# A decoder-layer kernel: other orders of the start-up work on ScalarE, VectorE and TensorE

## The chip, the core and the metric

The kernel runs on one core of a Trainium2 chip. The metric is the device time of one execution in microseconds; the median of 3 runs of the kernel before is 1664.91 us (1664.87 to 1665.24). All data are float32 but for a few masks.

## What is computed

One layer of a decoder on 1024 tokens of width 1024. First an RMSNorm, then projections, two attention mixers, a residual, a second RMSNorm, a mixture of 32 experts, a residual and a last RMSNorm. What the change touches is the first norm and the first use of its result:

```python
def rmsnorm(x, g):
    xf = x.astype(jnp.float32)
    y = xf * lax.rsqrt(jnp.mean(xf * xf, axis=-1, keepdims=True) + RMS_EPS)
    return y.astype(x.dtype) * g

hn = rmsnorm(h, norm_mix[l])
proj = xn @ w_in          # xn is hn; w_in is cut into blocks of 128 columns
```

## The kernel before

Each engine has its own instruction stream, written out by hand; semaphores order them. TT = 8 token tiles of P = 128 tokens are worked on one after the other in the head, and KT = 8 is the width in steps of 128.

The head, until the first projection, goes as follows. SyncE (SP) issues the loads in one queue: x tiles 0 to 3, the two halves of weight block 0, x tiles 4 and 5, weight block 1, x tiles 6 and 7, then further weights. GpSimd (POOL) makes constants (the identity `ident`, the column `eps_t` of epsilons, masks), and raises `const_ready` when the identity is done. ScalarE (ACT) waits for `const_ready`, then for each x tile takes the sum of squares (L885, with the read of the accumulator) and the root of the mean plus epsilon (L887, `std_done`). VectorE (DVE) takes the reciprocal (L1057), scales the tile into one of two buffers `xs` (L1060, `xs_ready`), and, when TensorE has turned the tile, takes it out of PSUM with the norm's gain into `hnT` (L1066, `hnT_done`). TensorE (PE) turns a scaled tile by 8 transposes of 128x128 (L555, `xT_ps`), in the function `turn_tokens`.

The order of VectorE's loop: for i = 0 to 8, scale tile i (if i < 8), then take tile i-1 (if i >= 1). Scaling tile i waits for `std_done` of tile i, and from i = 2 on for the transposes of tile i-2, since there are two `xs` buffers.

The order on TensorE: turn tiles 0 to 3; projection job 0 (L586; weight block 0 by tokens 0 to 511; 8 matmuls, each two instructions in the records, so 16), which waits for `hnT_done` of 4 tiles and for weight block 0; turn tiles 4 and 5; job 1 (weight block 1 by the same tokens, 16 instructions); turn tiles 6 and 7; job 2, which waits for all 8 tiles of `hnT`. From there on the projections follow one another (L586, L581), then attention, the output projection and the experts, whose matmuls (L834) have 64 stationary columns, two of them side by side at output partitions 0 and 64.

SyncE also waits for `xs_ready` of all 8 tiles before it issues the load of `w1c` (L420), which is first used some 100 us into the kernel.

Of the kernel before, what the change touches and what calls it, by code (L numbers as in the profile page):

```python
# [28 lines left out]
ALU = mybir.AluOpType  # L29
ACT = mybir.ActivationFunctionType  # L30
X = mybir.AxisListType.X

P = 128
# [10 lines left out]
TT = SEQ // P  # L44
KT = D // P
# [3 lines left out]
EPS = 1e-5  # L49
# [40 lines left out]
def build(nc, t, out):  # L90
    ctx = ExitStack()

    def sb(name, shape, dt=F32):
        return ctx.enter_context(nc.sbuf_tensor(name, shape, dt))

    def sem(name):
        return ctx.enter_context(nc.semaphore(name))
# [17 lines left out]
    def wa(a, b, pat=None, /, **kw):  # L115
        v = WA[:, a:b]
        return v.rearrange(pat, **kw) if pat else v

    def ba(a, b, pat=None, /, **kw):
        v = BA[:, a:b]  # L120
        return v.rearrange(pat, **kw) if pat else v

    hnT = wa(0, 8192, "p (k t) -> p k t", k=KT)
# [9 lines left out]
    xt = [wa(10496 + 1024 * i, 11520 + 1024 * i) for i in range(5)] + [wa(22528, 23552), wa(23552, 24576), ba(13312, 14336)]  # L133
# [8 lines left out]
    xs = ba(17408, 19456, "p (b n) -> p b n", b=2)  # L142
# [13 lines left out]
    ident = sb("ident", [P, P])  # L156
# [4 lines left out]
    gT = sb("gT", [P, KT])  # L161
# [10 lines left out]
    eps_t = sb("eps_t", [P, 1])  # L172
    stat = sb("stat", [P, 3, TT])
# [4 lines left out]
    esk = sb("esk", [P, 4, 2])  # L178
# [5 lines left out]
    PS = ctx.enter_context(nc.psum_tensor("PS", [P, 8, 512], F32))  # L184
# [6 lines left out]
        m_in0 m_in1 merge_ps gate_act merge_dve wout_in gff_in xr_in0 xr_in1 out_ps h2_done h2_std  # L191
        hn2_done h2T_ps h2T_done log_ps log_done zero_done routed scattered hn_st ids_in rows_due row_col row_ps row_tab ids_held slotx_done slots_done wr_in
        we0 we1 we2 we3 we4 we5 we6 we7 we8 x_blk x_tr xT_evac mm1 mm3 tanh_done hid_done hT_ps hT_done y_ps y_evac y_st
        g_in0 g_in1 fin_in0 fin_in1 fin_in2 fin_in3 fin_in4 fin_in5 fin_in6 fin_in7 g_in2 g_in3 g_in4 g_in5 g_in6 g_in7 comb_std comb_done out_st0 out_st1 act_step h2_st0 h2_st1 gate_in gw_in0 gw_in1 gst0 gst1 hu_done loop_left gelu_arg tanh_gates nsink_done comb_sum gfin_in assigned wdiag_done fin_ps wr_ready sel_done first_ps first_ids route_arg route_exp route_ps masks_ready tables y_free""".split()
    S = {n: sem(n) for n in names}
    block = ctx.enter_context(nc.Block())

# [8 lines left out]
    NBLK = len(blocks)  # L206

    jobs = [(name, c, hf) for c, (name, _, _) in enumerate(blocks) for hf in range(2)]
    jobs = [jobs[0], jobs[2], jobs[1], jobs[3]] + [("vg", 0, i) for i in range(TT)] + jobs[4:]
    job_of = {c: j for j, (name, c, h) in enumerate(jobs) if name != "vg" and h == 1}  # L210
# [60 lines left out]
    xT_ps = PS[:, 7, :].rearrange("p (c h n) -> p c h n", c=4, h=2)  # L271
# [268 lines left out]
    def _(pe):  # L540
# [8 lines left out]
        def turn_tokens(i):  # L549

            pe.wait_ge(S["xs_ready"], i + 1)
            if i >= 2:
                pe.wait_ge(S["hnT_done"], i - 1)
            for k in range(KT):
                mm = pe.transpose(PS[:, 4 + 2 * (i % 2) + k // 4, P * (k % 4):P * (k % 4) + P],  # L555
                                  xs[:, i % 2, P * k:P * k + P], ident[:, :])
            mm.then_inc(S["xT_ps"], 1)

        for i in range(4):
            turn_tokens(i)  # L560

# [11 lines left out]
        for j, (name, c, h) in enumerate(jobs):  # L573
# [3 lines left out]
            if name == "vg":  # L577
                if h == 0:
                    pe.wait_ge(S["vg_in"], 64)
                for k in range(KT):  # L580
                    mm = pe.matmul(PS[:, j % 4, 0:VG_W], hnT[:, k, P * h:P * h + P], vgw[:, k, :],  # L581
                                   start=(k == 0), stop=(k == KT - 1))
            else:
                pe.wait_ge(S[f"w_in{c % 6}"], 32 * (c // 6 + 1))
                for k in range(KT):
                    mm = pe.matmul(PS[:, j % 4, :], ws[:, c % 6, k, :], hnT[:, k, 512 * h:512 * h + 512],  # L586
                                   start=(k == 0), stop=(k == KT - 1))
# [11 lines left out]
            if j == 19:  # L599
                pe.wait_ge(S["gelu_dve"], 1)  # L600
                for ht in range(2):
                    mm = pe.matmul(PS[0:DH, 4, 0:126], w2c[:, 0, ht, :], gel[:, 2, 126 * ht:126 * ht + 126],
                                   start=(ht == 0), stop=(ht == 1))
# [122 lines left out]
        for dt in range(KT):  # L726
            for hf in range(2):
# [10 lines left out]
                for j, o in enumerate((qa, qb)):  # L738
                    for r in range(REP):
                        mm = pe.matmul(PS[:, b0 + j, :], wbr[:, dt % 2, 4 * j + r, :], o[:, r, sl],  # L740
                                       start=(r == 0), stop=(r == REP - 1))
# [120 lines left out]
        for j in range(TT // 2):  # L862
            i = 2 * j
# [5 lines left out]
            for c in range(2):  # L869
                for n in range(2):  # L870
                    mm = pe.matmul(PS[:, 2 * j + n, :], wdiag[:, j, c, :], fin_y[:, i, c, 512 * n:512 * n + 512],
                                   start=False, stop=(c == 1))
# [4 lines left out]
    def _(act):  # L877

        act.dma_start(gT[:, :], t["norm_mix"].rearrange("(k p) -> p k", p=P), allow_slow_non_contiguous=True) \
            .then_inc(S["gT_in"], 16)  # L880
        act.wait_ge(S["const_ready"], 1)

        for i in range(TT):
            act.wait_ge(S[f"x_in{i}"], 16)
# [91 lines left out]
        for i in range(TT + 1):  # L976
            if i >= 1:
                m = i - 1
# [64 lines left out]
    def _(dve):  # L1043
        steps = [0]

        def step(ins):

            steps[0] += 1
            ins.then_inc(S["dve_step"], 1)
            dve.wait_ge(S["dve_step"], steps[0])  # L1050


        dve.wait_ge(S["gT_in"], 16)
        for i in range(TT + 1):
            if i < TT:
                dve.wait_ge(S["std_done"], i + 1)
                step(dve.reciprocal(stat[:, 2, i:i + 1], stat[:, 1, i:i + 1]))  # L1057
                if i >= 2:
                    dve.wait_ge(S["xT_ps"], i - 1)
                dve.tensor_scalar(xs[:, i % 2, :], xt[i], stat[:, 2, i:i + 1], None, ALU.mult) \  # L1060
                    .then_inc(S["xs_ready"], 1)
            if i >= 1:
                m = i - 1
                dve.wait_ge(S["xT_ps"], m + 1)
                src = PS[:, 4 + 2 * (m % 2):6 + 2 * (m % 2), :].rearrange("p a (k n) -> p (a k) n", n=P)
                dve.tensor_tensor(hnT[:, :, P * m:P * m + P], src, gT[:, :].unsqueeze(2).to_broadcast([P, KT, P]),  # L1066
                                  ALU.mult).then_inc(S["hnT_done"], 1)

        def blocks_plus_pos(w):

# [129 lines left out]
        for pi in range(2 * KT):  # L1200
            b0, m, b, sl = 2 * (pi % 4), pi % 2, pi // 2 % 2, slice(512 * (pi % 2), 512 * (pi % 2) + 512)
# [56 lines left out]
        for i in range(TT + 1):  # L1258
# [5 lines left out]
            if i < TT:  # L1264
# [6 lines left out]
                src = PS[:, 2 * (i % 2):2 * (i % 2) + 2, :].rearrange("p a n -> p (a n)")  # L1271
# [15 lines left out]
        for k in range(5):  # L1287
            src, far_by = sums[k % 2], 2 ** k
# [60 lines left out]
        for n in range(TT + 1):  # L1349
# [4 lines left out]
            i = n - 1  # L1354
# [7 lines left out]
    def _(pool):  # L1362
        steps = [0]

        def step(ins):
            steps[0] += 1
            ins.then_inc(S["pool_step"], 1)
            pool.wait_ge(S["pool_step"], steps[0])

        g = nc.gpsimd  # L1370
        step(g.memset(ident[:, :], 0.0))
        step(g.memset(eps_t[:, :], EPS))
        step(g.memset(ones[:, :], 1.0))
        step(g.memset(tri[:, :], 1.0))
        step(g.memset(winmask[:, :], 0.0))
# [138 lines left out]
```

## Time and profile before

| | |
|---|---|
| median of 3 runs | 1664.91 us |
| the profiled execution | 1666.44 us |
| its span, first to last instruction | 1664.6 us |
| TensorE busy | 1561.5 us (94%) |
| VectorE, ScalarE, GpSimd busy | 559.3, 347.9, 295.4 us |
| mean granted clock of TensorE | 0.981 |
| start of job 0, job 2 in the span | 21.22, 42.42 us |

Times in the profile are microseconds from the start of the span. "Busy" on TensorE counts an instruction until its modelled end, so consecutive ones overlap; the distance from start to start tells the rate. The granted clock is 1.00 at 2.4 GHz and 0.50 at 1.2 GHz. The chain of waits follows what released each step, back from the end of the stretch.

### The profile page before, as it was taken

The page shows a single profiled execution, that of the slowest core. Times are in us where ns is not written, and L with a number is a line of the kernel's source. Part 1 is how long each engine was busy: PE and PEld are TensorE (multiplying, and loading weights), DVE is VectorE, ACT ScalarE, POOL GpSimd, SP SyncE. Part 2 cuts the span into 40 slices and gives each one's busy share as a digit, 9 for nine tenths or more (in the row PEclk, how much of TensorE's full clock was granted, in tenths as well). Part 3 has the DMA queues.
Part 4 walks back from the last instruction along what each step waited for, and adds up shares of the span by engine and source line. Part 5 has one row for each costly group of instructions (what it writes and reads, how often), then busy time and mean ns, then how long its engine had stood idle before and what let it go on. Part 6 is the DMA issues. An engine that isn't in the chain of part 4 may idle for free.

```text
span 1664.6 us, 21601 instructions
## 1 busy us (share of the span) xinstructions
PE 1561.5 (94%) x7605; PEld 841.6 (51%) x7606; DVE 559.3 (34%) x1538; ACT 347.9 (21%) x859; POOL 295.4 (18%) x434
## 2 busy tenths in 40 slices
PE   6999998999999999998999999699799999999995
PEld 3454544444444454444444555466366666666652
DVE  3201003766666656654222345411011111111115
ACT  3000002444343443433000111111111111111113
POOL 2000001322222222222001011221112121212113
PEclk9999999999999999998999999699999999999998
DMA  9205540453111111102443831599999999999938
GB/s 233 66 5 104 73 136 28 163 188 133 45 28 30 45 33 26 45 13 89 164 140 108 338 115 69 206 411 415 424 415 422 393 363 406 419 419 418 418 127 309
DMA packets 135977, 332.11 MB, mean 200 GB/s; under 512 B 39224, under 2 KB 79576, under 8 KB 126704
## 3 DMA queue, kind: packets, MB, share of 16 engines
q1 hardware_dynamic: 117472, 297.98, 49.1%
q0 software_dynamic: 10048, 21.32, 3.7%
q10 hardware_dynamic: 8400, 12.07, 2.1%
q8 instruction: 33, 0.54, 0.1%
q14 instruction: 24, 0.20, 0.0%
HBM read 276.09 MB, written 55.25 MB: 199 GB/s over the span
## 4 chain that ended last, share of the span: by engine, by line
PE 79%; DMA 8%; DVE 6%; issue 2%; ACT 1%; POOL 1%; SPq 1%; POOLq 0%; ACTq 0%; DVEq 0%
PE PS L834 15%; PE PS L702 12%; PE PS L586 11%; PE PS L848 8%; PE PS L740 7%; PE PS L775 6%; PE PS L688 4%; PE PS L649 4%; DMA WA<-w 4%; PE PS L668 4%; PE PS L581 3%; DMA BA<-hn_d,ids 1%; DMA ids<-ids_d 1%; PE PS L811 1%; PE PS L760 1%
## 5 line engine op out<-in xcount | busy, mean ns | idle before, releaser
L702 PE MATMUL PS<-WA 128*128 128x512 f32 x512 | 254.9, 611 | 2.2 <-ACT WA L944 1.6
L834 PE MATMUL PS<-WA,BA 128*64 128x256 f32 x2048 | 232.2, 384 | 4.7 <-DMA WA<-w 3.7
L834 PEld LDWEIGHTS PS<-WA,BA 128*64 128x64 f32 x2048 | 174.9, 139 | 69.3 <-issue 20.6
L586 PE MATMUL PS<-WA,BA 128*128 128x512 f32 x416 | 182.2, 599 | 5.4 <-DVE WA L1066 5.4
L1408 POOL TENSOR_SCALAR BA<-BA,rin,gates 128x640 f32<-128x640 f32 (+7 forms) x128 | 99.6, 781 | 270.7 <-DVE rin L1174 270.7
L1322 DVE SCALAR_TENSOR_TENSOR BA<-BA,PS 128x256 f32<-128x256 f32 x46 | 19.4, 421 | 347.1 <-ACT BA L1006 347.1
L586 PEld LDWEIGHTS PS<-WA,BA 128*128 128x128 f32 x416 | 79.3, 192 | 103.6 <-issue 97.7
L848 PE MATMUL PS<-WA,BA 128*64 128x512 f32 x512 | 117.8, 600 | 10.3 <-DVE BA L1332 8.4
L668 PEld LDWEIGHTS PS<-ident,BA 128*128 128x128 f32 x648 | 79.3, 144 | 94.1 <-issue 86.5
L702 PEld LDWEIGHTS PS<-WA 128*128 128x128 f32 x512 | 84.6, 190 | 78.5 <-issue 67.6
L934 ACT ACTIVATE BA<-PS,ngm 128x640 f32<-128x640 f32 (+7 forms) x128 | 89.9, 702 | 130.4 <-DVE ngm L1152 126.1
L775 PE MATMUL PS<-BA 128*128 128x512 f32 x256 | 113.1, 595 | 2.3 <-DVE BA L1210 2.3
L668 PE MATMUL PS<-ident,BA 128*128 128x128 f32 x648 | 101.2, 281 | 10.8 <-ACT BA L912 5.5
L740 PE MATMUL PS<-WA 128*128 128x512 f32 x256 | 110.1, 592 | 0.7 <-ACT WA L957 0.7
L834 PE MATMUL PS<-BA 128*64 128x256 f32 x896 | 99.7, 379 | 3.6 <-DMA BA<-w 3.6
L1184 DVE COPY BA<-PS 128x512 f32<-128x512 f32 (+3 forms) x126 | 62.7, 507 | 104.8 <-PE PS L668 104.7
L1151 DVE TENSOR_REDUCE mx<-PS 128x1 f32<-128x640 f32 (+7 forms) x128 | 90.6, 708 | 4.4
L834 PEld LDWEIGHTS PS<-BA 128*64 128x64 f32 x896 | 76.3, 137 | 30.4 <-issue 6.7
L1402 POOL TENSOR_TENSOR BA<-BA,rin 128x512 f32<-128x512 f32 (+1 forms) x32 | 31.5, 986 | 336.4 <-DVE rin L1161 336.4
L649 PE MATMUL PS<-WA 64*128 64x512 f32 (+3 forms) x384 | 75.8, 499 | 7.7 <-DVE pc L1142 4.0
L740 PEld LDWEIGHTS PS<-WA 128*128 128x128 f32 x256 | 48.6, 190 | 62.3 <-issue 60.7
L1474 POOL COPY ids<-ids 128x1 int32<-128x1 int32 x46 | 8.4, 183 | 399.6 <-PE PS L811 278.9
(238 smaller groups left out, 1524.9 us busy)
## 6 DMA issues: line engine op xcount, KB each, us to landing
WA<-w SPq DMA_DIRECT2D x66, 2048.0 KB, 24.9
BA<-w SPq DMA_DIRECT2D x30, 2048.0 KB, 27.9
rows_d<-WA SPq DMA_DIRECT2D x8, 2048.0 KB, 8.7
rows_d<-BA ACTq DMA_DIRECT2D x92, 128.0 KB
WA<-w_in SPq DMA_DIRECT2D x16, 512.0 KB, 5.4
gates_d<-WA SPq DMA_DIRECT2D x32, 256.0 KB, 2.4
WA<-gates_d SPq DMA_DIRECT2D x8, 1024.0 KB, 6.3
BA<-w_in SPq DMA_DIRECT2D x26, 256.0 KB, 5.6
```

The source lines that it names most:

```text
L586: mm = pe.matmul(PS[:, j % 4, :], ws[:, c % 6, k, :], hnT[:, k, 512 * h:512 * h + 512], start=(k == 0), stop=(k == KT - 1))
L649: mm = pe.matmul(PS[:, bank, 0:e - a], qb[rows, h, q], kz[rows, w, k0 + a:k0 + e], start=True, stop=True)
L668: mm = pe.transpose(PS[:, 4 + n % 2, P * m:P * m + P], src, ident[:, :])
L688: mm = pe.matmul(PS[DH * g:DH * g + DH, bank, :], v_sb[:, w, kb, DH * g:DH * g + DH], pT[:, SLOT0[br] + n, g, :, :], start=(br == "A" and ...
L702: mm = pe.matmul(PS[:, 6, :], gw[:, j, k, :], hnT[:, k, 512 * hf:512 * hf + 512], start=(k == 0), stop=(k == KT - 1))
L740: mm = pe.matmul(PS[:, b0 + j, :], wbr[:, dt % 2, 4 * j + r, :], o[:, r, sl], start=(r == 0), stop=(r == REP - 1))
L775: mm = pe.matmul(PS[:, 2 * (i % 2) + n, :], mT[:, i, k, :], wout[:, k, 512 * n:512 * n + 512], start=(k == 0), stop=(k == KT - 1))
L834: mm = pe.matmul(PS[DH * h:DH * h + DH, bank, 0:256], xT[:, k, :], w[par][:, k, 256 * h:256 * h + 256], start=(k == 0), stop=(k == KT - 1))
L848: mm = pe.matmul(PS[DH * n:DH * n + DH, 3, :], hT[:, j, SLOTS * h:SLOTS * h + SLOTS], W2[par][:, 2 * h + j, 512 * n:512 * n + 512], start= ...
L934: last = nc.scalar.activation(PB[:, n % 3, 0:nk], src, ACT.Exp, bias=ngm[:, v, 0:1], scale=SC, accum_out=den[:, v, 0:1])
L1151: step(dve.tensor_reduce(mx[:, v, 0:1], s[:, 0:nk], X, ALU.max))
L1408: last = g.tensor_scalar(pr, pr, rin[:, v, 0:1], gates[:, i, col:col + 1], ALU.mult, ALU.mult)
```

## The change

- GpSimd writes `eps_t` first, with a semaphore `eps_ready` of its own, ahead of the identity. ScalarE waits for this and no longer for `const_ready`, and takes one root of the epsilon column into a scratch element of `esk`, before it waits for the first x tile.
- TensorE, between `const_ready` and the first tile's transposes, multiplies the identity by itself: 6 rounds of 2 matmuls with 64 stationary columns, and 6 rounds of 4 with 32, each with 256 moving columns (the identity read twice), into a bank of PSUM that nothing else uses at that time. That is 36 matmuls.
- VectorE's loop is split. Tiles 0 to 3 are as before. From i = 4 on it takes tile i-1 first, and then scales tile i. The orders on the other engines stay.

```diff
+        wide = ident[:, :].unsqueeze(1).to_broadcast([P, 2, P])
+        for width in (64, 32):
+            for _ in range(6):
+                for c in range(0, P, width):
+                    pe.matmul(PS[c:c + width, 0, 0:2 * P], ident[:, 0:width], wide, start=True, stop=True)
         for i in range(4):
             turn_tokens(i)
...
-        act.wait_ge(S["const_ready"], 1)
+        act.wait_ge(S["eps_ready"], 1)
+        nc.scalar.activation(esk[:, 0, 0:1], eps_t[:, :], ACT.Sqrt)
...
-        for i in range(TT + 1):
-            if i < TT:
-                dve.wait_ge(S["std_done"], i + 1)
-                step(dve.reciprocal(stat[:, 2, i:i + 1], stat[:, 1, i:i + 1]))
-                if i >= 2:
-                    dve.wait_ge(S["xT_ps"], i - 1)
-                dve.tensor_scalar(xs[:, i % 2, :], xt[i], stat[:, 2, i:i + 1], None, ALU.mult) \
-                    .then_inc(S["xs_ready"], 1)
+
+        def scale_tokens(i):
+
+            dve.wait_ge(S["std_done"], i + 1)
+            step(dve.reciprocal(stat[:, 2, i:i + 1], stat[:, 1, i:i + 1]))
+            if i >= 2:
+                dve.wait_ge(S["xT_ps"], i - 1)
+            dve.tensor_scalar(xs[:, i % 2, :], xt[i], stat[:, 2, i:i + 1], None, ALU.mult).then_inc(S["xs_ready"], 1)
+
+        def take_tokens(m):
+
+            dve.wait_ge(S["xT_ps"], m + 1)
+            src = PS[:, 4 + 2 * (m % 2):6 + 2 * (m % 2), :].rearrange("p a (k n) -> p (a k) n", n=P)
+            dve.tensor_tensor(hnT[:, :, P * m:P * m + P], src, gT[:, :].unsqueeze(2).to_broadcast([P, KT, P]),
+                              ALU.mult).then_inc(S["hnT_done"], 1)
+
+        for i in range(4):
+            scale_tokens(i)
             if i >= 1:
-                m = i - 1
-                dve.wait_ge(S["xT_ps"], m + 1)
-                src = PS[:, 4 + 2 * (m % 2):6 + 2 * (m % 2), :].rearrange("p a (k n) -> p (a k) n", n=P)
-                dve.tensor_tensor(hnT[:, :, P * m:P * m + P], src, gT[:, :].unsqueeze(2).to_broadcast([P, KT, P]),
-                                  ALU.mult).then_inc(S["hnT_done"], 1)
+                take_tokens(i - 1)
+        for i in range(4, TT):
+            take_tokens(i - 1)
+            scale_tokens(i)
+        take_tokens(TT - 1)
...
         g = nc.gpsimd
+        g.memset(eps_t[:, :], EPS).then_inc(S["eps_ready"], 1)
         step(g.memset(ident[:, :], 0.0))
-        step(g.memset(eps_t[:, :], EPS))
```

## Rows read from the trace of the kernel before

**Rows 1.** The page: the chain of work that ended last, by engine.
```profile
PE 79%; DMA 8%; DVE 6%; issue 2%; ACT 1%; POOL 1%; SPq 1%; POOLq 0%; ACTq 0%; DVEq 0%
```

**Rows 2.** Chain of waits, 12 to 24 us; columns: start, us, what.
```profile
6.24 11.31 DMA WA<-x
...
19.28 0.75 DVE BA L1060
20.03 1.14 DVE WA L1066
...
21.22 2.93 PE PS L586 x3
```

**Rows 3.** Chain of waits, 24 to 60 us.
```profile
30.48 1.75 PE PS L555 x16
...
39.10 0.89 PE PS L555 x8
...
40.01 2.37 DVE WA L1066 x2
...
42.42 14.00 PE PS L586 x32
```

**Rows 4.** Timeline of ACT; columns: start, us, instruction, [idle before, releaser].
```profile
4.70 1.28 ACT L885 ACT_TABLE_LOAD   x1 [4.70 <-DMA WA<-x]
...
7.16 1.28 ACT L887 ACT_TABLE_LOAD   x1
...
8.66 1.04 ACT L885 ACTIVATE BA<-WA 128x1024 f32<-128x1024 f32 x1
```

**Rows 5.** Timeline of DVE.
```profile
10.15 0.17 DVE L1057 RECIPROCAL stat<-stat 128x1 f32<-128x1 f32 x1 [0.15 <-ACT stat L887]
...
12.12 1.22 DVE L1066 TENSOR_TENSOR WA<-PS,gT 128x1024 f32<-128x1024 f32 x1 [0.92 <-PE PS L555]
...
13.45 0.75 DVE L1060 TENSOR_SCALAR BA<-WA,stat 128x1024 f32<-128x1024 f32 x1
14.12 1.22 DVE L1066 TENSOR_TENSOR WA<-PS,gT 128x1024 f32<-128x1024 f32 x1
...
16.11 1.22 DVE L1066 TENSOR_TENSOR WA<-PS,gT 128x1024 f32<-128x1024 f32 x1
```

**Rows 6.** Timeline of PE: the head, and two short stretches at 11.3 and 16.6 us.
```profile
10.15 3.65 PE L555 MATMUL PS<-ident,BA 128*128 128x128 f32 x16 [10.15 <-DVE BA L1060]
14.27 1.57 PE L555 MATMUL PS<-ident,BA 128*128 128x128 f32 x8 [0.47 <-DVE BA L1060]
16.26 1.09 PE L555 MATMUL PS<-ident,BA 128*128 128x128 f32 x8 [0.42 <-DVE BA L1060]
...
11.24 1.06 PE L555 MATMUL PS<-ident,BA 128*128 128x128 f32 x4
...
16.42 0.82 PE L555 MATMUL PS<-ident,BA 128*128 128x128 f32 x6
```

**Rows 7.** PE busy and granted clock by stretch; the clock stands after the count.
```profile
18.00:18.50 0.50, 0.00 (x0) 1.00 1.27 282
18.50:19.00 0.50, 0.00 (x0) 0.71 1.34 231
...
25.50:26.00 0.50, 0.50 (x2) 0.96 1.18 325
...
41.00:42.40 1.40, 0.00 (x0) 1.00 1.00 327
42.40:44.00 1.60, 1.58 (x4) 1.00 1.06 336
```

**Rows 8.** Timeline of POOL: the last step of the identity.
```profile
3.07 0.29 POOL L1378 TENSOR_SCALAR_AFFINE_SELECT ident<-ident 128x128 f32<-128x128 f32 x1 [0.24 <-POOL cmpmask L1377]
```

**Rows 9.** Chain of waits, 1100 to 1120 us: a run of 64-column matmuls.
```profile
1111.72 6.91 PE PS L834 x64
```

**Rows 10.** DMA, issues at 2.32, 3.38, 11.56 and 24.01 us: KB, us to landing.
```profile
WA<-x SPq DMA_DIRECT2D x1, 512.0 KB, 8.7
...
BA<-w_in SPq DMA_DIRECT2D x1, 256.0 KB, 12.9
...
BA<-w_in SPq DMA_DIRECT2D x1, 256.0 KB, 9.7
...
BA<-w_in SPq DMA_DIRECT2D x1, 96.0 KB, 6.5
```

More of the change, by code:

```diff
@@ L193, in build @@
         we0 we1 we2 we3 we4 we5 we6 we7 we8 x_blk x_tr xT_evac mm1 mm3 tanh_done hid_done hT_ps hT_done y_ps y_evac y_st
-        g_in0 g_in1 fin_in0 fin_in1 fin_in2 fin_in3 fin_in4 fin_in5 fin_in6 fin_in7 g_in2 g_in3 g_in4 g_in5 g_in6 g_in7 comb_std comb_done out_st0 out_st1 act_step h2_st0 h2_st1 gate_in gw_in0 gw_in1 gst0 gst1 hu_done loop_left gelu_arg tanh_gates nsink_done comb_sum gfin_in assigned wdiag_done fin_ps wr_ready sel_done first_ps first_ids route_arg route_exp route_ps masks_ready tables y_free""".split()
+        g_in0 g_in1 fin_in0 fin_in1 fin_in2 fin_in3 fin_in4 fin_in5 fin_in6 fin_in7 g_in2 g_in3 g_in4 g_in5 g_in6 g_in7 comb_std comb_done out_st0 out_st1 act_step h2_st0 h2_st1 gate_in gw_in0 gw_in1 gst0 gst1 hu_done loop_left gelu_arg tanh_gates nsink_done comb_sum gfin_in assigned wdiag_done fin_ps eps_ready wr_ready sel_done first_ps first_ids route_arg route_exp route_ps masks_ready tables y_free""".split()
     S = {n: sem(n) for n in names}
```

## The prediction

> **What bounds the kernel now.** First the page's chain: TensorE carries 79% of it, so a microsecond that TensorE loses or gains in the head reaches the end, unless something later waits for a clock time of its own [rows 1]. Then the chain of waits of the head, to see who lets job 0 start. Before 17.55 it is the load of x tile 4 (issued 6.24, landing 11.31 later), and behind it VectorE: it scales tile 4 (19.28), and only then takes tile 3 (20.03); job 0 starts at 21.22 [rows 2]. But tile 3 had been turned by 16.26 + 1.09 = 17.35 [rows 6]. So VectorE's wait for the root of tile 4 stands ahead of work that job 0 needs. In the next stretch TensorE is without a gap: job 0, tiles 4 and 5 turned from 30.48 in 1.75, job 1, tiles 6 and 7 turned from 38.94 (the chain's 39.10 is the last 8 transposes' share), two takes at 40.01 for 2.37, job 2 at 42.42 [rows 3]. What counts is how much earlier or later job 2 starts; from there 32 instructions take 14.00, 0.4375 each, with no wait [rows 3]. The last weights of the group that comes next were landed at 24.01 + 6.5 = 30.5 [rows 10], so an earlier job 2 would find its data.
>
> The clock is the other thing. Four transposes at 11.24 take 1.06, six at 16.42 take 0.82: start to start 213 and 109 ns, the two levels of 1.2 and 2.4 GHz [rows 6] (the clock column shows 1.00 in both, so it is no evidence before its first change). The rise lies inside the burst of 14.27, some 5 us after TensorE's first work. The clock falls at about 18.65, 1.3 us after the last transpose, and rises at about 25.5, 4.3 us after job 0 began [rows 7]. Job 0 and the half level: from 21.22 to 30.3 it takes 9.1, against 16 x 0.4375 = 7.0 at full level; the fall costs 2.1.
>
> **Root of the epsilon column, `eps_ready`.** ScalarE loads a table for the square (4.70, 1.28) and another for the root (7.16, 1.28), both behind x tile 0; the second square, at 8.66, needs no load [rows 4]. So the root's table serves both, and loaded from about 1.5 on it is ready before the first tile at 4.7. From a square's start to the reciprocal it takes 10.15 - 8.66 = 1.49 [rows 4, 5]: tile 0 has its root at 6.2 and not at 8.7, and TensorE could turn it at about 7.6. Tile 3 lands at 2.32 + 8.7 = 11.0 [rows 10], root at 12.5, 0.1 before now. GpSimd's memset moves by one place: nothing on the path.
>
> **Work on the identity.** It stands ahead of the transposes in TensorE's own stream, so it delays them if it lasts beyond 7.6. It begins when the identity is there, at 3.36 plus a signal [rows 8], say 3.6. 36 matmuls are 72 instructions, since float32 ones show as two. Of those with 64 columns, 64 take 6.91, 108 ns each, two side by side [rows 9]: 24 x 0.108 = 2.6 at full level. With 32 columns no row stands. Upper bound: also 108 each, 48 x 0.108 = 5.2; lower bound: four side by side, 54 each, 2.6. I take the lower, since from one to two side by side the rate doubles just so (512 columns alone 437, hence 256 alone 219, against 108). By the Trainium skill (TensorEngine Tiling (Array Packing), Available Configurations) an array cut to 32 columns works as four tiles, which gives the same 2.6; no run here shows it. Sum 5.2 at full level and 10.3 at half. It begins at half, as the first transposes did. With a rise after 4.3 to 5.1 us of work, as in the two rises above, at about 8.4, 2.4 of the 5.2 are done, and 2.8 remain: end E = 11.2. Bounds: 10.1 with an earlier rise, 13.9 with none. That is later than the 7.6 at which tile 0 is ready, and 1.05 later than TensorE's first transpose now; the root's gain of 2.5 is swallowed.
>
> **From E to job 0.** Tile 0 is out 1.09 after E [rows 6]; takes then follow 2.0 apart (12.12, 14.12, 16.11) and a scaling starts 1.33 after a take, the turning 0.82 after that (13.45 to 14.27) [rows 5, 6]. Take 1 at E + 3.1, scaling 3 at E + 4.4, tile 3 turned at E + 5.25 to E + 6.35, take 3 at once, since it no longer stands behind scaling 4; job 0 1.25 later (19.95 to 21.22, with the take itself): E + 7.6 = 18.8. Weight block 0 is there at 3.38 + 12.9 = 16.3 [rows 10], no bound. Gain: 21.22 - 18.8 = **2.4**; its ends are 3.5 (E = 10.1) and 0.0 or slightly below (E = 13.9).
>
> **Take before scale, for tiles 5 and 7.** This is what the same edit costs. TensorE's order is unchanged: turn 4 and turn 5 behind job 0. Now tile 5 is scaled long before. After the change it is scaled only after take 4, and take 4 waits for turn 4, which waits for job 0. Turn 4 out after 1.09, take to scaling 1.33, scaling to turning 0.82: turn 5 starts 3.24 after turn 4 and not 0.87 [rows 5, 6]. **2.35** lost, TensorE idle, with job 1 queued behind it. The same for tiles 6 and 7 behind job 1: now job 2 starts 3.48 after turn 6 (38.94 to 42.42) [rows 3]; then 3.24 to turn 7, 1.09, and take 7 with 1.25: 5.6. **2.1** lost. Tiles 4 and 6 are scaled during take 3's end and job 1. The w1c load, behind the eighth scaling, goes some 4 us later; its first use is far off. Weight block 1 is there at 11.56 + 9.7 = 21.3 [rows 10], before job 1 at about 31.
>
> **The clock after it.** Job 0: between E and 18.8 TensorE has tiles 0 and 1 together, then one turning in each 2.0, then 1.3 idle, the pattern that led to the fall at 18.65. So I expect job 0 to pay its 2.1 as now: 0. Now the clock holds from turn 7 to job 2, with 1.4 idle at 41.00 to 42.40 [rows 7]. After the change tiles 6 and 7 stand as two bursts of 0.9 with 2.35 and 1.4 idle around the second, emptier than what led to the fall at 18.65. I take one more fall, at the price of job 0's, **2.1**, paid by job 2. The gap between turns 4 and 5 is single, between two full jobs, and may bring another (0 to 2.1); taken at 0.
>
> The Trainium skill (TensorE: Matmul & The Clock Gate, Part 4: PE-mode transpose) says that the full clock doesn't engage for transposes. This trace differs: with nothing but transposes since 10.15 the spacing went from 213 to 109 ns. By the page the tiles between E and job 0 could never hold the clock, and the rival "the clock holds" below would be out; the sum would stay.
>
> **Sum.** -2.4 + 2.35 + 2.1 + 2.1 = +4.2 us. Against the profiled execution, 1666.44 to 1670.6; it lies 1.5 above the median of the runs shown, and against that, 1664.91 + 4.2 = **1669.1**. The measurement can tell 0.2%, 3.3 us, from no change; the forecast is beyond it, by little.
>
> **The rivals.**
> - *Stalls without a new fall* (24%). The two handed-over waits cost 4.45 and the earlier job 0 gives 2.4, but the clock stays up over the gaps: +2.0, 1667.0, within 0.2%. For it: the clock held over the 1.4 at 41.0. Against it: the fall at 18.65, after a burst and 1.3 idle. It turns into the forecast as soon as one job runs at half level.
> - *The identity work keeps the clock up to job 0* (13%). Then job 0 takes 7.0: 2.1 less than the forecast, +2.1, 1667.0; with no fall later either, 0. Against it: all of that work is over 7.6 us before job 0.
> - *The identity work is long* (13%): 32-column matmuls don't run four at a time, or the clock stays at half for them. E = 13.8 and not 11.2: all of the 2.4 is gone, +6.8; with transposes at half level too, 0.9 more. 1671.7 to 1672.6.
> - *The head gains and the stalls aren't paid* (5%). If turn 5 and turn 7 did not wait (scaling overlapped in a way that I don't see) the 4.45 would go: -2.4, and with job 0 at the full clock -4.5: 1660.4, faster by over 0.2%.
> - The forecast itself (45%), 1668.3 to 1671.5, its upper end with a fall after the first gap too.
>
> **Numbers.** Slower by over 0.2%: 45 + 13 = 58%. Within: 24 + 13 = 37%. Faster: 5%. The range for 8 in 10 reaches from 1664.5 (E at 10.1 and no fall) to 1672.0 (long identity work or a second fall); left out are the faster case and the ends of the others.
>
> **What would show it.** In the changed kernel's profile: one table load on ScalarE, before 4; the first reciprocal at about 6.3; 72 matmuls from about 3.6 to 11.2, their distance halving under way; VectorE's fourth take ahead of the scaling of tile 4, job 0 at 18.8; gaps of 2.35 between turns 4 and 5 and turns 6 and 7, ended by VectorE's scaling; job 2 at about 44.5 against 42.42; granted clock 0.50 in part of job 2. It is wrong if the second turn of a pair follows the first at once, if job 2 starts before 42.4, or if job 2 is later but the end of the span is not.

## The result, and the profile after

The changed kernel takes 1668.19 us (median of 22 runs, 1665.06 to 1673.22) against 1664.88 for the kernel before in as many runs: the ratio is 1.002, 95% interval 1.0011 to 1.0028, or +3.3 us (+1.8 to +4.7). Single runs of one kernel lie several microseconds apart, so each ratio below has its interval, and the head, which is the kernel's first 60 us or so, is read from the profiles. The profiled execution took 1669.43, with a span of 1667.7 (before: 1666.44 and 1664.6).

VectorE and ScalarE of the changed kernel, timeline; start, us, instruction:

```profile
1.46 1.28 ACT L887 ACT_TABLE_LOAD   x1 [1.46 <-PEq L1518]
...
6.54 0.16 DVE L1064 RECIPROCAL stat<-stat 128x1 f32<-128x1 f32 x1 [6.54 <-DMA gT<-norm_mix]
...
15.53 2.50 DVE L1073 TENSOR_TENSOR WA<-PS,gT 128x1024 f32<-128x1024 f32 x2
...
26.12 1.23 DVE L1073 TENSOR_TENSOR WA<-PS,gT 128x1024 f32<-128x1024 f32 x1 [6.18 <-PE PS L555]
27.26 0.15 DVE L1064 RECIPROCAL stat<-stat 128x1 f32<-128x1 f32 x1
27.45 0.75 DVE L1067 TENSOR_SCALAR BA<-WA,stat 128x1024 f32<-128x1024 f32 x1
```

There is one table load, over long before the first tile, where rows 4 had two behind it. Takes 2 and 3 follow each other at 15.53; take 3 no longer stands behind the scaling of tile 4 as in rows 2. But at 26.12 VectorE, idle for 6.18, gets turn 4 from TensorE, and only behind that take does it scale tile 5.

TensorE of the changed kernel, timeline. The second row is the same view of a shorter stretch, 8 to 8.5 us: the first of the 32-column matmuls.

```profile
3.35 7.13 PE L563 MATMUL PS<-ident 128*64 128x256 f32 x72 [3.35 <-POOLq L1396]
...
7.68 1.07 PE L563 MATMUL PS<-ident 128*32 128x256 f32 x16
...
10.40 1.97 PE L555 MATMUL PS<-ident,BA 128*128 128x128 f32 x16
13.67 1.09 PE L555 MATMUL PS<-ident,BA 128*128 128x128 f32 x8 [1.30 <-DVE BA L1067]
15.67 1.09 PE L555 MATMUL PS<-ident,BA 128*128 128x128 f32 x8 [0.90 <-DVE BA L1067]
18.08 7.13 PE L591 MATMUL PS<-WA,BA 128*128 128x512 f32 x16 [1.32 <-DVE WA L1073]
25.05 1.04 PE L555 MATMUL PS<-ident,BA 128*128 128x128 f32 x8
28.26 1.09 PE L555 MATMUL PS<-ident,BA 128*128 128x128 f32 x8 [2.18 <-DVE BA L1067]
29.19 7.03 PE L591 MATMUL PS<-WA,BA 128*128 128x512 f32 x16
36.06 1.04 PE L555 MATMUL PS<-ident,BA 128*128 128x128 f32 x8
39.27 1.09 PE L555 MATMUL PS<-ident,BA 128*128 128x128 f32 x8 [2.17 <-DVE BA L1067]
41.68 16.91 PE L591 MATMUL PS<-WA,BA 128*128 128x512 f32 x32 [1.32 <-DVE WA L1073]
```

And PE busy with the granted clock (after the count) where it fell and rose:

```profile
40.50:41.00 0.50, 0.00 (x0) 0.74 0.79 229
...
47.50:48.00 0.50, 0.50 (x2) 0.93 0.00 0
```

Read against rows 3 and 6: job 0 starts 3.14 earlier (18.08 for 21.22) and takes 6.97 to the next transposes and not 9.10, with no fall of the clock before it. TensorE now rests 1.32 before job 0, where it rested 3.87 in the kernel before. Then the bracketed waits of 2.18 and 2.17 on VectorE's scaling (L1067), which the kernel before doesn't have: turn 4 to job 1 takes 4.14 and not 1.75, turn 6 to job 2 takes 5.62 and not 3.48. Job 2 starts at 41.68, and so 0.74 *earlier* than before. But now the clock falls at about 40.7, in the rest before job 2, and jobs 2 and 3 take 16.91 where rows 3 have 14.00. They end at 58.59 and not 56.42. In order, the terms are the earlier job 0, its full clock, the two waits, and the fall before job 2: -3.14 - 2.13 + 2.39 + 2.14 + 2.91 = +2.17.

### The profile page after: what moved, and what is told of

Its sections match the earlier page's. It is cut to its first block, busy times and chain, and to the rows that moved or that the text cites. A ratio compares the mean times of both kernels' runs of the same rounds, so it can differ in the third digit from the quotient of the medians.

```text
span 1667.7 us, 21743 instructions
## 1 busy us (share of the span) xinstructions
PE 1571.8 (94%) x7677; PEld 843.3 (51%) x7678; DVE 559.6 (34%) x1538; ACT 347.4 (21%) x859; POOL 296.1 (18%) x434
## 4 chain that ended last, share of the span: by engine, by line
PE 80%; DMA 7%; DVE 6%; issue 3%; ACT 1%; POOL 1%; SPq 1%; POOLq 0%; ACTq 0%; DVEq 0%
PE PS L839 15%; PE PS L707 12%; PE PS L591 11%; PE PS L853 8%; PE PS L745 7%; PE PS L780 6%; PE PS L693 4%; PE PS L654 4%; DMA WA<-w 4%; PE PS L673 4%; PE PS L586 3%; DMA ids<-ids_d 1%; PE PS L816 1%; PE PS L765 1%; PE PS L573 1%
## 5 line engine op out<-in xcount | busy, mean ns | idle before, releaser
L673 PE MATMUL PS<-ident,BA 128*128 128x128 f32 x648 | 100.7, 280 | 11.3 <-ACT BA L918 5.5
```

The source lines that it names most:

```text
L673: mm = pe.transpose(PS[:, 4 + n % 2, P * m:P * m + P], src, ident[:, :])
```

## The experiments

The figure of merit in the head is the time at which jobs 2 and 3 are done; from there on the kernels are alike. "Clock low from" is the first half microsecond in which the granted clock was below 1.00 in the profiled execution. Each ratio is against runs of the kernel before that were made beside it; 5 to 12 runs stand behind each experiment (5 behind e6 and e8), and 22 behind the changed kernel. Times in the head are those of one profile each.

| kernel | job 0 | job 2 | jobs 2, 3 done | clock low from | ratio to before (95%) |
|---|---|---|---|---|---|
| before | 21.22 | 42.42 | 56.42 | 18.5 | 1 |
| changed | 18.08 | 41.68 | 58.59 | 40.5 | 1.0020 (1.0011 to 1.0028) |
| e1 take 3 alone early, with root and identity | 18.00 | 37.08 | 51.08 | none | 0.9985 (0.9973 to 0.9997) |
| e2 whole new order alone | 18.66 | 43.95 | 60.96 | 29.5, 43.0 | 1.0015 (1.0002 to 1.0028) |
| e3 changed, no identity work | 16.67 | 40.35 | 56.93 | 38.5 | 1.0004 (0.9991 to 1.0017) |
| e4 changed, three fills | 19.13 | 44.40 | 58.40 | 19.0 | 1.0019 (1.0007 to 1.0032) |
| e5 identity work alone | 20.68 | 41.44 | 55.44 | 20.5 | 1.0001 (0.9990 to 1.0012) |
| e6 take 3 early, root, no identity work | 16.67 | 35.74 | 49.74 | none | 0.9954 (0.9941 to 0.9967) |
| e7 as e1, 4 rounds for 6 | 16.57 | 37.34 | 51.34 | 16.5 | 0.9969 (0.9955 to 0.9982) |
| e8 before, with a delay | 20.64 | 52.78 | 66.78 | 20.5 | 1.0071 (1.0057 to 1.0085) |
| e9 root alone | 21.20 | 43.30 | 57.30 | 17.0 | 0.9996 (0.9985 to 1.0007) |
| e10 take 3 early alone | 18.66 | 37.73 | 51.73 | none | 0.9969 (0.9958 to 0.9981) |
| e11 as e6, three fills | 16.67 | 35.74 | 49.74 | none | 0.9968 (0.9957 to 0.9980) |
| e12 changed, six fills | 17.83 | 41.44 | 55.44 | none | 1.0003 (0.9993 to 1.0013) |

### Which half of VectorE's order costs, which gives: e1, e2, e10

e1 is the changed kernel with this loop; e10 puts the same loop alone into the kernel before; e2 puts the change's whole loop alone into the kernel before.

```diff
-        for i in range(4, TT):
-            take_tokens(i - 1)
-            scale_tokens(i)
+        take_tokens(3)
+        scale_tokens(4)
+        for i in range(5, TT):
+            scale_tokens(i)
+            take_tokens(i - 1)
         take_tokens(TT - 1)
```

> The change, but only tile 3 is taken ahead of the scaling of tile 4; tiles 5, 6 and 7 are scaled ahead of the take before them, as in the kernel before. Theory of the two handed-over waits: the gaps of 2.18 and 2.17 us between turns 4 and 5 and turns 6 and 7 of the changed kernel are gone, turns 4+5 and 6+7 take 1.8 each, job 0 still starts at 18.1, job 2 at about 37.3 (changed kernel 41.7, before 42.4), the clock stays at 1.00 up to job 2, and jobs 2 and 3 take 14.0 and not 16.9. In all -7.3 us against the changed kernel, -5 against the kernel before, some 1660. Rival (the head's times don't reach the end; the loss is made later, in the last gathers): 1667 to 1669, as the changed kernel.

> The kernel before with VectorE's new order alone; no early root, no work on the identity. Theory: job 0 starts at 18.6 and not 21.2, at the half clock as in the kernel before, so that it ends at 27.7; then the two gaps; job 2 at 44.4, after a fall of the clock that costs jobs 2 and 3 another 2.9: +4.9 us against before, 1669.8. Rival (the order is harmless or good, and the work on the identity brings the loss): -2.6 or so, 1662.

> The kernel before with tile 3 taken ahead of the scaling of tile 4, and nothing else: the half of VectorE's new order that I hold to be the gain. Theory: job 0 at 18.7 and not 21.2 or 20.7, turns in pairs without gaps, job 2 at 37.7 to 39.7, no fall of the clock before job 2: -2.5 to -4, some 1662. With the whole new order it was 1667.7, +2.6. Rival (the order of tiles 5 to 7 doesn't matter): +2 to +3, as with the whole order.

e1, timeline of TensorE: both pairs of turns run as 16 transposes without a wait, and jobs 2 and 3 take 14.00.

```profile
18.00 7.13 PE L591 MATMUL PS<-WA,BA 128*128 128x512 f32 x16 [1.32 <-DVE WA L1073]
24.98 1.91 PE L555 MATMUL PS<-ident,BA 128*128 128x128 f32 x16
...
33.59 1.91 PE L555 MATMUL PS<-ident,BA 128*128 128x128 f32 x16
37.08 14.00 PE L591 MATMUL PS<-WA,BA 128*128 128x512 f32 x32 [1.57 <-DVE WA L1073]
```

e2, the same view: the waits of 2.17 and 2.18 are there without any other part of the change, and the clock fell behind the first of them too, so that job 1 takes 8.36 to the next turn and not 6.87 as in the changed kernel.

```profile
18.66 7.13 PE L586 MATMUL PS<-WA,BA 128*128 128x512 f32 x16 [1.32 <-DVE WA L1066]
25.64 1.04 PE L555 MATMUL PS<-ident,BA 128*128 128x128 f32 x8
28.85 1.33 PE L555 MATMUL PS<-ident,BA 128*128 128x128 f32 x8 [2.17 <-DVE BA L1060]
29.97 8.53 PE L586 MATMUL PS<-WA,BA 128*128 128x512 f32 x16
38.33 1.04 PE L555 MATMUL PS<-ident,BA 128*128 128x128 f32 x8
41.55 1.09 PE L555 MATMUL PS<-ident,BA 128*128 128x128 f32 x8 [2.18 <-DVE BA L1060]
```

The heads ended as expected to 0.4 us (51.08 for 51.3, 60.96 for 61.3, job 2 of e10 at 37.73), though e2's by another way: I had put its first fall before job 0, and it came a job later. Timed, e10 is 0.9969 where the whole order alone is 1.0015. The intervals are far apart: one edit, two halves of opposite sign. Tile 3 early gives 5 us; tiles 5 and 7 behind the takes cost 6 (changed kernel against e1) to 8 (e2 against e10). Timed, e1 (0.9985) gained less than the 0.9970 that I expected, e2 lost 2.5 us where I expected 4.9, and e10 gained 5.2 where I expected 2.5 to 4.

### What the clock's fall before job 2 is worth: e4, e12

Both keep the change and its waits, and put work on the identity into the rests: e4 with the first hunk below, e12 with both.

```diff
                 turn_tokens(4 + 2 * j)
+                fill(4)
                 turn_tokens(5 + 2 * j)
+            if j == 1:
+                fill(2)
...
         for i in range(4):
             turn_tokens(i)
+            fill((0, 2, 1, 2)[i])
```

`fill(n)` is n rounds of two 64-column matmuls of the identity by itself, as in the change, into a bank that no job uses yet.

> The change with more work on the identity in the gaps: 4 rounds of two 64-column matmuls (1.7 us at full clock) between turns 4 and 5 and between turns 6 and 7, and 2 rounds (0.9 us) ahead of job 2. It separates the gaps from the fall of the clock after them. Theory: the gaps and the start of job 2 (41.7 to 41.9) stay, the clock stays at 1.00, jobs 2 and 3 take 14.0 and not 16.9: -2.9 us against the changed kernel, 1665.3, level with the kernel before. Rival (what makes jobs 2 and 3 slow is not TensorE's idleness but a collision with the loads): 16.9 stays, 1668.

> The changed kernel with the fills between turns 4 and 5, turns 6 and 7 and ahead of job 2, as in the run with these alone, and besides with 2, 1 and 2 rounds behind turns 1, 2 and 3, ahead of job 0. The run with the first three fills was as slow as the changed kernel, its profile with a fall ahead of job 0 in place of the one ahead of job 2. Theory: with fills in all rests no job runs at the half clock, in any execution; both gaps stay; job 0 at 18.1 to 19, job 2 at 41.7 to 42.7, jobs 2 and 3 done at 55.7 to 56.7: 1664 to 1665, some 3 us under the changed kernel and level with the kernel before. Rival (the falls cost less on average than in the profiles shown, or the clock falls all the same): 1667 or more.

e4, TensorE's timeline and the clock. The rests behind job 0 are filled and jobs 2 and 3 take 14.00 behind the same waits: so their 16.91 was the clock, not the loads beside them. But in this execution the identity work took 8.19, and the clock fell at 19 and made job 0 long instead (8.64 to the next turn).

```profile
3.34 8.19 PE L563 MATMUL PS<-ident 128*64 128x256 f32 x72 [3.34 <-POOLq L1405]
...
19.13 8.80 PE L597 MATMUL PS<-WA,BA 128*128 128x512 f32 x16 [1.32 <-DVE WA L1082]
27.77 1.04 PE L555 MATMUL PS<-ident,BA 128*128 128x128 f32 x8
...
39.74 1.95 PE L568 MATMUL PS<-ident 128*64 128x256 f32 x16
41.99 1.09 PE L555 MATMUL PS<-ident,BA 128*128 128x128 f32 x8 [0.30 <-DVE BA L1076]
43.02 1.08 PE L568 MATMUL PS<-ident 128*64 128x256 f32 x8
44.40 14.00 PE L597 MATMUL PS<-WA,BA 128*128 128x512 f32 x32 [0.30 <-DVE WA L1082]
```

```profile
19.00:19.50 0.50, 0.37 (x1) 0.61 1.48 244
```

Timed, e4 was as slow as the changed kernel (1.0019): a miss. e12 left no long rest before job 0 either. Its profile has the clock at 1.00 throughout the head, and its job 2:

```profile
41.44 14.00 PE L598 MATMUL PS<-WA,BA 128*128 128x512 f32 x32 [0.30 <-DVE WA L1083]
```

Its time is 1.0003, against 1.0020 of the changed kernel: 2.8 us less, as expected, though the two intervals still overlap by 0.0002. So with the waits kept and the clock held the kernel is level with the kernel before: the waits use up what the earlier job 0 gives, and what the change loses is about what the falls cost.

Over all profiles the falls before job 2 go with the waits. With a short burst between rests of 2.17 or 2.18 and 1.32 (changed kernel, e2, e3) the clock fell each time. With the two turns together and one rest of 1.57 (before, e1, e5, e6, e7, e9, e10) it never did, nor with the rests filled (e4, e12). The single gap between turns 4 and 5 brought a fall in e2 alone of the three.

### What the identity work and the root do: e3, e5, e6, e7, e9, e11

e3 and e6 are the changed kernel and e1 without the matmuls ahead of the first turn; e5 and e9 are the kernel before with these alone, and with the root alone; e7 is e1 with `range(4)` for `range(6)`; e11 is e6 with `fill((0, 0, 1, 2)[i])` behind turn i and `fill(2)` ahead of job 2.

> The change without the work on the identity. Theory that this work holds TensorE's clock through job 0 at the price of a later first tile: tile 0 is turned at 8.1 and not 10.5, at the half clock; job 0 starts at 16.6 to 17.5 and not 18.1, but takes about 9.1 and not 7.0, so that it ends about 1.3 us later than in the changed kernel; with both gaps and the fall before job 2 the same: 1669.5. Rival (that work only delays the tokens): job 0 takes 7.0 all the same and the kernel gains 1 us on the changed one, 1667.

> The kernel before with the work on the identity alone, ahead of the first transposes. Theory: the work runs from 3.4 to 10.4; VectorE still takes tile 3 only behind the scaling of tile 4, so job 0 starts at 21.2 as before whatever the first tiles do. What can be gained is the clock of job 0, and by the run without that work, where job 0 was at the full clock all the same, TensorE's 3.9 us of rest ahead of job 0 decide that more than the work: 0 to -2, 1663 to 1665. Rival (the work is what makes the changed kernel slower): +2 or more, 1667.

> The early root, and tile 3 taken ahead of scaling tile 4, but tiles 5 to 7 scaled ahead of the takes before them, and no work on the identity. Theory: job 0 at 16.7 as in the run without that work, turns 4+5 and 6+7 without gaps, job 2 at 35.7, jobs 2 and 3 done at 49.7: 1.4 us ahead of the run with the identity work (51.1) and 6.7 ahead of the kernel before. Timed, with job 0 now and then at the half clock: 1660 to 1662. Rival (the work on the identity pays): 1663 or more.

> As the run that takes only tile 3 early, with 4 rounds and not 6 of either width of the work on the identity. Theory: it lasts from 3.35 to about 8.3 (measured spacings 213 ns, then 108 and 54), so tile 0, scaled at 8.0, is turned at once; job 0 at 16.3 to 16.7, job 2 at 35.6, done with jobs 2 and 3 at 49.6, with a clock that is up from before the first tile: 1660 to 1661. Rival: no difference from the run with 6 rounds, 1662.4, because something else than the first turn sets job 0.

> The kernel before with the early root of the epsilon column alone. Theory: tile 0 is turned at 8.1 and not 10.2, but tile 3 is still taken behind the scaling of tile 4, whose load lands at 17.5: job 0 at 20.7 to 21.2 and job 2 at 41.4 to 42.4 as before, 0 to -1 us, by the clock of job 0 alone. Rival (the root's 2.5 us reach job 0): -2, 1663.4 or less.

> The early root and tile 3 taken early, tiles 5 to 7 as before, and the work on the identity not ahead of the first tile but in rests that are there anyway: 1 round of two 64-column matmuls after turn 2, 2 rounds after turn 3, 2 rounds ahead of job 2. Theory: job 0 at 16.7, at the full clock in each run and not in most, job 2 at 35.7 and never behind a fall: 1657.5 to 1659, the best of all. Rival (the clock isn't kept by them, or they get in the way): 1659 to 1661.

e3, TensorE's timeline: without the identity work turn 0 starts at 8.15, job 0 at 16.67, and job 0 is at the full clock all the same.

```profile
8.15 3.59 PE L555 MATMUL PS<-ident,BA 128*128 128x128 f32 x16 [8.15 <-DVE BA L1062]
12.27 1.10 PE L555 MATMUL PS<-ident,BA 128*128 128x128 f32 x8 [0.53 <-DVE BA L1062]
14.26 1.09 PE L555 MATMUL PS<-ident,BA 128*128 128x128 f32 x8 [0.89 <-DVE BA L1062]
16.67 7.13 PE L586 MATMUL PS<-WA,BA 128*128 128x512 f32 x16 [1.32 <-DVE WA L1068]
```

My expectation for e3, that job 0 would pay with the half clock, failed: the head ended at 56.93, 1.7 before the changed kernel's, and the time was 1.0004 and not 1.0028. The same step from e1 to e6 takes the ratio from 0.9985 to 0.9954, with intervals apart. So the identity work is a loss of its own once take 3 is early. How large it is stays open: the heads of e1 and e6 differ by 1.3, the timed ratios by 5 us, and e7, whose head is no shorter than e1's, timed 0.9969. In the head it costs the 2.3 us by which turn 0 comes later (10.40 for 8.15, of which 1.3 to 1.4 reach job 0), and it doesn't hold the clock to job 0 reliably: e4 and e5 had it and fell at 19.0 and 20.5, e7 at 16.5. e5 alone does nothing (1.0001), because take 3 still waits for tile 4: job 0 at 20.68. Nor does the root alone (0.9996): turn 0 at 8.15, job 0 at 21.20. It only makes the rest before job 0 longer, 5.84 and not 3.87, and in its profile job 0 takes 9.99 to the next turn. The root's 2 us become worth something only when take 3 is early (e10's job 0 at 18.66, e6's at 16.67).

e9, the same view:

```profile
21.20 10.16 PE L586 MATMUL PS<-WA,BA 128*128 128x512 f32 x16 [5.84 <-DVE WA L1067]
31.19 1.91 PE L555 MATMUL PS<-ident,BA 128*128 128x128 f32 x16
```

e7's head, whose fall at 16.5 gave back what the shorter work had gained:

```profile
8.69 1.09 PE L555 MATMUL PS<-ident,BA 128*128 128x128 f32 x8
...
16.57 8.83 PE L591 MATMUL PS<-WA,BA 128*128 128x512 f32 x16 [1.31 <-DVE WA L1073]
```

e11's fills did not get in the way, as its timeline shows:

```profile
15.28 1.08 PE L565 MATMUL PS<-ident 128*64 128x256 f32 x8
16.67 7.13 PE L595 MATMUL PS<-WA,BA 128*128 128x512 f32 x16 [0.30 <-DVE WA L1079]
```

But they brought nothing that the runs can tell: 0.9968 against 0.9954 of e6, with overlapping intervals, and 1659.61 us where I expected 1657.5 to 1659. e6's own profile has no fall in the head that they could have saved.

### Does the head's time reach the end: e8

```diff
                 turn_tokens(5 + 2 * j)
+            if j == 1:
+                fill(30)
```

> The kernel before with 30 rounds of two 64-column matmuls on the identity ahead of job 2 and nothing else: 60 matmuls, 120 instructions of 108 ns, 12.9 us, of which 1.5 stand in for the wait for take 7. It measures how much of a delay of job 2 reaches the end. Theory (TensorE's chain carries everything from there on): job 2 at 53.9 and not 42.4, +11.5 us, 1676.5. Rival (a part of the head's time is given back later, which would explain that the timed differences are about half of those in the head of the profiles): +5 to +8.

e8, chain of waits, 36 to 62 us:

```profile
38.01 1.75 PE PS L555 x16
39.75 13.10 PE PS L565 x120
```

Job 2 starts at 52.85 by the chain and 52.78 by the timeline, 10.4 to 11.3 behind where it stands in profiles of the same order (42.42 in the kernel before, 41.44 in e5); the time rose by 0.71%, 11.8 us (9.5 to 14.2). Within that interval the whole delay arrives. Gains arrive too: e10's head is 4.7 shorter and its time 5.2 (3.2 to 7.0), e6's 6.7 and 7.7 (5.5 to 9.8). That timed differences of e1 and e2 (-2.5, +2.5) were smaller than those of their heads (-5.3, +4.5) is therefore hardly a later stage giving back. A profile shows one execution, and which rest the clock falls in differs between executions; that this makes the difference for e1 and e2 is not shown.

## Why the prediction was right, and where not

It said +4.2 us, 1669.1, slower by a little; measured were +3.3, 1668.19, within the range. The mechanism of the loss, the two handed-over waits and the fall behind the second, was right. That the sum is this close is in part luck: one term was wrong by 2.1, two others by 0.7 and 0.8, and they partly cancel. One of the prediction's own signs of being wrong came true, "if job 2 starts before 42.4": it started at 41.68, because job 0 kept its clock. By its steps:

- *The reach of job 0* was forecast at 18.8, 2.4 gained; it was 18.08, 3.1. The rule "E + 7.6" held to the hundredth (10.47 + 7.6); the identity work ended at 10.47 and not 11.2, since it began at 3.35 and not 3.6 and the clock rose earlier, some 3.5 us into the work (first 32-column matmul at 7.68, where it would be 8.5 at the half clock). The lower bound taken for the 32-column matmuls, 54 ns, was right: 48 of them from 7.68 to turn 0 at 10.40 are 57 ns each, and read start to start within that stretch (8 of them from 9.21 to 9.64) it is 54. The Trainium skill (TensorEngine Tiling (Array Packing), Available Configurations) has an array cut to 32 columns work as four tiles; the trace agrees, for that is a quarter of the 219 that the prediction estimates for 256 columns alone.
- *The handed-over waits*, 2.35 (its own 3.24 - 0.87 is 2.37) and 2.1: the extra time was 2.39 and 2.14, the idle before the second turn 2.18 and 2.17, ended by VectorE's scaling, as the prediction named it. e1, e2 and e10 show that this half of the order does it.
- *The fall before job 2* came, behind the two rests that the prediction named, and e2 and e3 had it there too. Its size was off: 2.9 and not 2.1. The term was taken from job 0 of the kernel before, where the clock had been low for some time and rose 4.3 into the job; here it rose nearly 6 into jobs 2 and 3. The price of a fall is no constant: in the profiles it is 1.5 to 3.0, by how much of the work runs before the clock rises again.
- *The clock of job 0* was the wrong step: "I expect job 0 to pay its 2.1 as now". It paid nothing in this profile. The prediction counted the rest of 1.3 before job 0 as the same pattern that had led to the fall at 18.65; but in the kernel before that rest goes on to 3.87, and the early take cuts it to 1.32. With a rest of 3.3 to 5.8 before job 0 the clock fell in all four profiles (before, e5, e8, e9), with 1.32 in two (e4, e7) of eight. The effect is that of the rival at 13%, the identity work keeping the clock up, but its mechanism isn't borne out: e2, e3, e6 and e10 had none of that work and held the clock through job 0, e4 and e7 had it and did not. With job 0's clock, its start and the size of the fall put right, the sum is +4.2 - 2.1 - 0.7 + 0.8 = +2.2, against the +2.17 of the profiles' heads.
- *From the head's +2.2 to the span's +3.1.* The long middle, up to the last transposes of the experts (1616.53 in the kernel before, 1617.91 in the changed one), took 0.8 less, and from there to the last sums of gathered rows (start 1651.14 and 1654.29) it took 1.8 more. Both stretches are the same code in all fourteen kernels, and over their profiles the first differs by up to 4.9 us and the second by up to 2.7. So one pair of spans can't resolve the change, and what of the 1.1 between the head's 2.2 and the timed 3.3 is the change's stays open.
- *"Stalls without a new fall"* was priced at +2.0; e12 is that case, made on purpose: head -1.0, time +0.5 (-1.2 to +2.2). It is lower because job 0 kept its clock as well, which the prediction put at "with no fall later either, 0".
- On the clock and transposes the prediction weighed the Trainium skill (TensorE: Matmul & The Clock Gate, Part 4: PE-mode transpose), which says that they don't engage the full clock. e3 has nothing but transposes before job 0, and its turns go from 3.59 for 16 with the wait between to 1.10 for 8. The measurement decides: here they do.
- *The range.* Its lower end, 1664.5, doesn't come out of what it names: E at 10.1 and no fall before job 2 give 1665.9, with job 0 at the full clock besides 1663.8. The measured time lies far from either.

The best versions take tile 3 early, and no other tile: e6, with the root, 0.9954 (0.9941 to 0.9967), median 1658.37; alone it is e10, one move of a line, 0.9969 (0.9958 to 0.9981). With 5 and 7 runs behind them, and intervals that overlap, the two are not told apart.

## What to carry to other kernels

When two engines hand buffers back and forth, reorder one tile at a time and write down, for each tile, what the other engine is doing when the moved step is due: taking tile 3 early removed a wait for a load, while the same swap for tiles 5 and 7 put VectorE's scaling behind a transpose that stood behind a whole job. Count a gap on TensorE twice, once for its length and once for the clock that may fall in it: here 2.2 and 1.3 us of rest around one short burst cost 2.9 more. Check first whether the reordered step ends a long rest: in this kernel the early take did, and job 0 kept its clock. Work that is meant to keep the clock belongs into rests that exist (e12), and pays only where the clock would have fallen (e11 gained nothing that the runs can tell); ahead of the first real work it is a delay.

## What the runs showed of the hardware that was not expected

- TensorE's clock before its first change is not what the granted clock column prints: 1.00 in all profiles, with matmuls spaced at the half level ([rows 6] and e3's first turns, 16 in 3.59 with a wait between).
- The same instructions found the clock falling in one execution and not in the next: the changed kernel held it up to 40.5, the same kernel with fills that come only after job 0 (e4) let it fall at 19.0, before the first of them. One profile is one draw, and a verdict on the clock needs timed runs.
